# Reordering the end of the last scan and the start of the attention projections in a two-block language model kernel

## The reference, cut to what matters

```python
# second mixer (gated linear attention), 4 heads, 64-token chunks
o = gla_chunked(q, k, v, gk)                 # S carried from chunk to chunk
o = gated_rmsnorm(o, norm_w, gate)
x = layer_norm(DEEP_ALPHA * x + o.reshape(...) @ w_out, ln_g[1], ln_b[1])
# second block
h = concatenate([zeros, meta_tokens, x])
hn = rms_norm(h, attn_norm_g)                # h * rsqrt(mean(h*h)) * g
proj = hn @ w_in                             # 3524 columns
```

## Time and profile before

| what | value |
|---|---|
| median of three runs | 3591.52 us (3590.5 to 3592.09) |
| profiled execution, its own time | 3595.09 us |
| its span in the trace | 3593.4 us |
| mean granted TensorE clock | 0.968 of full |
| PE busy, of the span | 94% |
| DVE, ACT, POOL busy | 45%, 31%, 13% |

### The profile page before, as it was taken

One profiled execution on the slowest core, in us unless ns is written; L12 is line 12 of the kernel. 1 busy time (PEld: TensorE's weight loads), 2 busy tenths in 40 slices (PEclk: granted clock), 3 DMA queues, 4 the chain that ended last, 5 costly groups with the idle time before them and its releaser, 6 DMA issues.

```text
span 3593.4 us, 46846 instructions
## 1 busy us (share of the span) xinstructions
PE 3372.3 (94%) x19401; PEld 2568.2 (71%) x19401; DVE 1623.6 (45%) x3386; ACT 1122.4 (31%) x2273; POOL 458.4 (13%) x729
## 2 busy tenths in 40 slices
PE   8999999999999989999978999899999999999997
PEld 6775876677587657757736688678844588888886
DVE  3533444353344444534551699766721333323324
ACT  3432342243234323313342223366600211111112
POOL 0210111021011242203251122000000000000000
PEclk9999999999999999999987999999999999999999
DMA  2210100101010101101111123200040011111111
GB/s 97 71 36 12 41 20 23 36 25 37 10 41 16 48 15 42 42 16 38 54 62 60 36 88 94 94 1 1 1 188 12 30 48 47 59 47 47 47 47 47
DMA packets 40079, 159.61 MB, mean 44 GB/s; under 512 B 5335, under 2 KB 10009, under 8 KB 34362
## 3 DMA queue, kind: packets, MB, share of 16 engines
q1 hardware_dynamic: 39866, 156.62, 13.1%
HBM read 136.68 MB, written 19.92 MB: 44 GB/s over the span
## 4 chain that ended last, share of the span: by engine, by line
PE 78%; DVE 13%; ACT 4%; POOL 2%; issue 2%; DMA 1%; SPq 0%; POOLq 0%; ACTq 0%; DVEq 0%
PE pp L552 8%; PE pp L554 8%; PE pp L553 8%; PE pp L1185 7%; PE pp L1186 7%; PE pp L1187 7%; PE pp L722 5%; DVE xT L2230 4%; PE pp L1167 3%; PE pp L1157 3%; PE pp L873 3%; PE pp L1124 2%; PE pp L1108 2%; DVE arena L2230 2%; PE pp L652 1%
## 5 line engine op out<-in xcount | busy, mean ns | idle before, releaser
L552 PE MATMUL pp<-gx_hi,pw_hi 128*128 128x512 f32 x1584 | 651.8, 411 | 29.5 <-DVE pw_lo L1785 28.7
L554 PE MATMUL pp<-gx_hi,pw_lo 128*128 128x512 f32 x1584 | 628.6, 397 | 0.0
L553 PE MATMUL pp<-gx_lo,pw_hi 128*128 128x512 f32 x1584 | 628.1, 397 | 0.0
L552 PEld LDWEIGHTS pp<-gx_hi,pw_hi 128*128 128x128 f32 x1584 | 304.3, 192 | 102.6 <-DVE pw_lo L1785 31.8
L554 PEld LDWEIGHTS pp<-gx_hi,pw_lo 128*128 128x128 f32 x1584 | 303.6, 192 | 66.8
L553 PEld LDWEIGHTS pp<-gx_lo,pw_hi 128*128 128x128 f32 x1584 | 304.8, 192 | 59.0
L1185 PE MATMUL pp<-x_hi,wt_hi 128*128 128x512 f32 x704 | 274.1, 389 | 1.1 <-DVE x_lo L2359 1.1
L1187 PE MATMUL pp<-x_hi,wt_lo 128*128 128x512 f32 x704 | 273.9, 389 | 0.0
L1186 PE MATMUL pp<-x_lo,wt_hi 128*128 128x512 f32 x704 | 273.9, 389 | 0.0
L722 PE MATMUL pp<-xT,arena 128*128 128x512 f32 x512 | 233.8, 593 | 6.3 <-DVE arena L1961 6.3
L1785 DVE TENSOR_TENSOR pw_lo<-arena,pw_hi 128x1024 fp32r<-128x1024 f32 x73 | 89.6, 1229 | 241.8 <-ACT pw_hi L1240 241.8
(11 more groups left out here) (436 smaller groups left out, 6073.6 us busy)
## 6 DMA issues: line engine op xcount, KB each, us to landing
arena<-in_tiles_dram SPq DMA_DIRECT2D x73, 512.0 KB, 3.6
arena<-in_units_dram SPq DMA_DIRECT2D x33, 1024.0 KB, 4.8
xT<-in_tiles_dram SPq DMA_DIRECT2D x27, 512.0 KB, 3.7
xT<-in_w_outs_dram SPq DMA_DIRECT2D x6, 2048.0 KB, 8.5
arena<-gates_scratch SPq DMA_DIRECT2D x16, 512.0 KB, 4.6
gates_scratch<-arena SPq DMA_DIRECT2D x11, 512.0 KB, 5.1
arena<-in_xT_dram SPq DMA_DIRECT2D x8, 512.0 KB, 8.2
y<-in_x_dram SPq DMA_DIRECT2D x1, 4096.0 KB, 14.6
```

Of the source, the lines that this page charges most:

```text
L552: mm(b[:, hs], wh[:, c], X[0][:, k, hs], k == 0, False)
L553: mm(b[:, hs], wh[:, c], X[1][:, k, hs], False, False)
L554: m = mm(b[:, hs], wl[:, c], X[0][:, k, hs], False, k == 7)
```

## The change

Nothing is computed differently. Instructions move within the orders of the engines, and some PSUM banks are others:

- POOL, steps n = 3 to 7 of group 5: `norm2(n-3)` ahead of `layer_rstd(n-1)`; at step 8 too, where the row is 5.
- POOL and ACT, block part: `split(74)` comes first.
- DVE: `layer_affine(5)` and `(6)` move from behind the scan into step 8, between `gated(7)` and the two `add_half(7)`.
- PE: `norm2(4)` (`hT(4)`) moves ahead of the last output matmuls; `norm2(5)` moves between the first half of tile 73 and that of tile 74.
- PSUM: tile 74 gets pair 3 (banks 6 and 7) instead of pair 1; `hT` of rows 6, 7 and the meta transposes go on around banks 2 to 5 instead of 6 and 7; small products and tile 76 move accordingly.

```diff
@@ PE
+                if g == 5 and n == 8:
+                    norm2(4)
                 for hf in range(2) if n else ():
                     b = place_(R["f"], ("op", g, n - 1, hf), ("y", g, n - 1, hf))
...
-                if g == 5 and n >= 4:
+                if g == 5 and 4 <= n < 8:
                     norm2(n - 4)
...
-            got = [place_(Ring([i], True), ("proj", 73 + i), (("ikfc",), ("iqc", 0))[i]) for i in range(2)]
+            got = [place_(Ring([0], True), ("proj", 73), ("ikfc",)), place_(Ring([3], True), ("proj", 74), ("iqc", 0))]
             for hf in range(2):
                 for i in range(2):
                     run(half(73 + i, got[i], hf))
+                    if hf == 0 and i == 0:
+                        norm2(5)
                     if hf == 1 and i == 0:
-                        meta_feature(73, Ring([7]))
+                        meta_feature(73, Ring([2]))
                 if hf == 0:
-                    R["n"] = Ring([6, 7])
-                    for n in range(5, 8):
+                    for n in range(6, 8):
                         norm2(n)
...
-            index_keys(2, [-1], Ring([6]))
+            index_keys(2, [-1], Ring([3]))
             run(steps)
-            run(whole(76, [1], ("akc",)))
-            meta_feature(76, Ring([7]))
+            run(whole(76, [3], ("akc",)))
+            meta_feature(76, Ring([2]))
@@ ACT
+            split(74)
             layer_scale(7, "lb")
             spread(4)
...
             norm2(6)
-            split(74)
@@ DVE
                 if n < 8:
                     head_scale(g, n, ob2)
+                if g == 5 and n == 8:
+                    layer_affine(5)
+                    layer_affine(6)
                 for hf in range(2) if n else ():
                     add_half(g, n - 1, hf)
...
-            for n in range(5, 8):
-                layer_affine(n)
+            layer_affine(7)
@@ POOL
+                if g == 5 and n >= 3:
+                    norm2(n - 3)
                 if g == 5 and n:
                     layer_rstd(n - 1, "lb")
-                if g == 5 and n >= 3:
-                    norm2(n - 3)
...
+            split(74)
             po.wait_ge(ended(6))
...
             norm2(6)
-            split(74)
             norm2(7)
```

## The result

The changed kernel took 3563.78 us (median of four runs, 3563.02 to 3568.95), the kernel before 3591.01 beside it (four runs, 3586.3 to 3592.09). The ratio is 0.993, 95% interval 0.9913 to 0.9947: 27.2 us faster. The forecast was 3568.0, range 3560.5 to 3573. The profiled execution took 3563.36 us, with a span of 3561.6 and a mean granted clock of 0.972 (0.968 before). Measured again (after_b), the same kernel took 3565.66 us (3561.02 to 3575.57, six runs) against 3592.13, ratio 0.9933 [0.992, 0.9946].

A forecast was written before the change was run, and what follows sets the result against it. PE's idle stretches at the seam, 16.19 and 14.73 us, were taken as the bound. Gains of 22.0 us at the second halves plus 1.6 make 23.6; off the median of 3591.5 that gives 3568 us, range 3560.5 to 3573.

The forecast's parts named there:

- waits of `obT`, steps 5 and 6: PE's two waits for the DVE-POOL loop, 0.79 and 0.77 us, close with POOL's root moved ahead: 1.6 us.
- clock at the last output matmuls: PE's last output matmuls keep their low stretch, 0.58 for 4 us, despite the moved transposes: 0 us gained.
- from their end to the first halves: Tile 73's first matmul waits for row 3 instead of row 4, starting at 1869.3 instead of 1882.75: 13.4 us earlier.
- from first to second halves: On PE, about 19.6 us instead of 28.1, as row 5's transposes come earlier; 22.0 us gained by the second halves.
- behind the second halves: After the seam the orders are the same and all engines come out together, so nothing more is gained.
- `hT(4)` just fits: Row 4's transposes fit ahead of PE's last output matmuls with 0.2 us to spare, cost 0; if late, 1.9 us lost.
- DVE has room for the affines: In step 8, between gated(7) and the last add_half, DVE fits the affines of rows 5 and 6: cost 0.
- all four low stretches: Low clock stays at the output matmuls, first halves, second halves and around 1922, behind the 16-column products; no gain counted.
- The clock stays high: High clock at one or more low stretches; two or more save 3.5 to 7.6 us: 3560 to 3565 us, chance 0.22.
- Transposes did not raise the clock: PE, 1902.87 to 1910.89: busy 5.10 of 8.02 us with transposes, clock 0.50; so moved transposes buy no clock.
- new wait: ACT, behind with row 6, delays the second halves to 1898.3; gain 12.6 + 1.6, 3577 us, chance 0.10.
- the low clock: Clock stays at 0.50 from the first half on through tiles 73 to 76: 32 us lost, 3600 us, chance 0.02.

The follow-up runs named there:

- u_banks: Kernel after with tile 74 back in banks 2 and 3 and transposes of rows 6, 7 in banks 6 and 7: 3570.88 us, ratio 0.9945.
- u_root: Kernel after with POOL's root of the mean square behind the statistics again in steps 3 to 8: 3572.78 us, ratio 0.995.
- u_aff: Kernel after with DVE's affines of rows 5 and 6 back behind the scan: 3572.81 us, ratio 0.9948.
- u_split: Kernel after with the split of tile 74 back behind norm2(6) on ACT and POOL: 3570.28 us, ratio 0.9947.
- imp1: Kernel after with gx_lo of row 3 ahead of DVE's last additions, row 6's affine behind row 7's statistics, and other moves: 3561.22 us, ratio 0.992.
- imp2: Kernel after, reordered around the last scan: both affines stay in step 8, gx_lo of row 3 ahead of the additions, ACT reordered: 3557.15 us, ratio 0.9908.
- u_ht4: Kernel after with row 4's transposes back behind the last output matmuls: 3569.15 us, ratio 0.9933.
- u_ht4_b: Second measurement of the kernel after with row 4's transposes back behind the last output matmuls: 3568.59 us, ratio 0.9936.
- o_banks: Kernel before with the new PSUM banks alone: 3580.84 us, ratio 0.9974.

## Why the prediction was right, step by step

Measured over the profiled pair, counted within the traces.

| step | predicted | measured |
|---|---|---|
| waits of `obT`, steps 5 and 6 | 1.6 | 2.0 (the lead of 6.4 at step 4 is 8.4 at the last output matmuls) |
| clock at the last output matmuls | 0 | 1.7 (8.80 to 7.13) |
| from their end to the first halves | 13.4 | 13.6 (17.07 to 3.43) |
| from first to second halves | 8.6 | 9.6 (28.14 to 18.57) |
| behind the second halves | 0 | 1.0 (42.85 to 41.86 until the `rb` matmuls; 2.0 in the repeat, 40.82) |
| sum | 23.6 | 27.9 |

The medians give 27.2. The remaining 3.9 of the profiled pair's 31.8 us are no part of the change: 6.4 us were there by step 4, and 2.5 are lost again behind the `rb` matmuls, 1.5 of them up to the threshold search (89.3 against 87.8). The structure held in every step: which wait ended last at each place (u_banks), that `hT(4)` just fits, and only because POOL's root goes ahead (u_root; the step took 12.25 us against 12.34 before), that DVE has room for the affines (it still waits 0.82 us for PE's matmuls ahead of its last addition) and that row 7 needs them early (u_aff), that ACT must have tile 74's split early (u_split), and that ACT is nearly full between the halves. Row 7's squares were put 9.1 us behind the first halves and came 8.9 behind; row 5's `spread` 12.3 and 12.0.

What was mis-sized is the clock. The forecast let all four low stretches stand, a term of 0, and the profiled pair has 1.7 us at the output matmuls and 1.0 behind the second halves. 3563.8 lies just below the forecast's own band of 3565 to 3572, in that of the rival "The clock stays high"; the repeat, 3565.66, lies in the forecast's band. The rival came true by half: the low stretch at the output matmuls went, that of the first halves shrank without any gain at the second, and of the last two one went and one stayed, which ones depends on the trace. The 23.6 us that the mechanism gave came within 4.3 of the measured sum; what the clock adds to it is in part luck, since it differs between traces of one kernel.

The step that failed is "Transposes did not raise the clock", taken from a stretch in which PE was already low and idle in between. That transposes did not bring a low clock back there says nothing on whether they help to hold a high one. By the Trainium skill ("TensorE: Matmul & The Clock Gate", PE-mode transpose) they don't count as PE activity in the same way; 8.80 without and 7.13 with them, in both pairs, speaks against the use that was made of that rule here, and the two traces with 8.83 in spite of them keep it open. Whether it is their columns or only the shorter idle pieces (2.11 and 0.32 us, against 3.94 in one) wasn't separated.

The remaining 1.0 between the halves is ACT's: the prediction let it wait between the three `spread`, and it ran 6.40 us in one piece. One cost had no term at all: DVE's affines and POOL's split block each other (below). The affines of rows 5 and 6 took 5.9 us instead of the 4.9 that were reckoned, and it fitted because DVE had time to spare.

The other rivals: no new wait took the gain, although leaving out the banks, `hT(5)`, the affines, the split or the early root each brought one; the low clock ended after 3.4 us at the first halves and 5.4 at the second. The time was not given back: in the profiled pair the search's first count starts 32.9 us earlier, and the end comes 31.8 earlier.

## What to carry to other kernels

When several late things stand behind one wait, undoing one edit at a time and making one edit alone give different prices (the banks alone left 5.3 of 13.6 us at the second halves; undoing them lost 11.8): work out what is late next before counting a gain. Where two engines look independent, look at what their instructions read at the same moment: a POOL instruction of 0.57 us on a serial chain took 1.52 beside one of DVE here. And compare within a trace, from an event ahead of the edit to one behind it, where single spans differ by more than the effect; and look at a second trace of the same kernel before a level of the clock is put down to an edit.

## What the hardware did that was not expected

**DVE and POOL block each other.** Two rows of DVE and two of POOL of the kernel after:

```profile
1848.32 2.24 DVE L2115 TENSOR_TENSOR y<-y,arena 128x1024 f32<-128x1024 f32 x1
...
1860.77 2.10 DVE L2115 TENSOR_TENSOR y<-y,arena 128x1024 f32<-128x1024 f32 x1 [0.86 <-ACT y L1350]
```

```profile
1847.12 2.36 POOL L2561 TENSOR_TENSOR pe_lo<-masks,pe_hi 128x1024 fp32r<-128x1024 f32 x1
...
1859.41 2.37 POOL L2561 TENSOR_TENSOR pe_lo<-xT,pe_hi 128x1024 fp32r<-128x1024 f32 x1
```

The affine instruction takes 1.21 us where POOL is idle and 2.24 and 2.10 here. In both places POOL's split was running when it started, and it ended 1.1 us behind POOL's end: it did nearly all of its 1.21 us of work only then. In u_split, with POOL idle at the affine of row 7, that instruction took 1.22. The other way round, POOL's one-column instructions in imp1 took 1.08 and 1.52 us instead of 0.23 and 0.57 beside DVE's affines, and in the kernel after, at 1853.10, the first one of row 5's root took 1.17 instead of 0.19. The Trainium skill ("SBUF — State Buffer", "Who interferes with whom") calls this port pair an exclusive lock between a VectorE instruction with two SBUF inputs and a GpSimd one that reads SBUF; the traces agree. It costs the kernel after nothing in these places as far as its rows show: DVE has slack at 1848, ACT stands 2.44 us for row 7's root at 1859.49 behind all that row 5's could delay, and it comes to the squares of row 7 only at 1867.87, long after the affine's end. In imp1 it cost 1.8 us at the root of row 7's statistics and more at row 6's, most of what the new order was to bring; imp2 bears this out, though it moved other instructions too.

**The clock** was low at the first halves behind 3.4 us of idle time (0.55 in the kernel after) and stayed at 1.00 behind 2.55 (u_ht4, u_ht4_b, o_banks) and 0.83 (imp2). Elsewhere the same code got either level behind the same idle time: row 6's output matmuls behind 2.20 us, the second halves of after and after_b behind 1.40. On 16 output matmuls the levels differ by 1.7 us, as much as leaving out `hT(4)` cost. What decides between them stays open here.
